# Gates one unit later, keys copied by two engines, and the last tile in two halves of columns, in a two-layer streaming encoder step

## The chip, the cores and the metric

The kernel runs on 1 core of one Trainium2 chip. The metric is the device time in microseconds (us) of one execution; the median over several executions is given. The engines are named as the profile names them: PE is TensorE, PEld its weight loads, DVE is VectorE, ACT is ScalarE, POOL is GpSimd, SP is the engine whose queue issues most DMAs.

## The reference, cut to what matters

```python
def mixer_layer(h, p, pos, ckv_past, krope_past, conv_past, ...):
    z = rmsnorm(h, ln_in) @ w_in
    c_q, c_kv, k_r, g_a, u_val, u_gate, g_c = jnp.split(z, [...], axis=-1)
    q = (rmsnorm(c_q, ln_q) @ w_q_b).reshape(b, t, 8, 96)      # 64 plain + 32 rotated
    ckv_new = rmsnorm(c_kv, ln_kv)
    # keys and values of a head come from ckv_new through w_kv_b; block-causal softmax
    y_a = rmsnorm(o_a * jax.nn.silu(g_a), ln_out_a)
    u = u_val * jax.nn.sigmoid(u_gate)
    v = causal_dwconv(u_pad, conv_w, conv_b)                   # 31 taps
    v = jax.nn.silu(layernorm(v, ln_conv_g, ln_conv_b))
    y_c = rmsnorm(v * jax.nn.silu(g_c), ln_out_c)
    h = h + jnp.concatenate([y_a, y_c], axis=-1) @ w_out
    gate = jax.nn.sigmoid(rmsnorm(h, ln_pg) @ w_pg)
    return h + gate * (p @ w_pe), ckv_new, kr_new, conv_state
# two layers, over a prompt group (512 frames) and a sample group (8 x 16 frames with a
# cache of 256), then y = rmsnorm(h, ln_f)
```

## The kernel before

**Tiles.** The 640 token rows lie in five tiles of 128 (`t` 0 to 3 the prompt, 4 the samples). Each product with a weight matrix is formed in chunks `c` of 256 input rows (two `k` of 128). A weight chunk is split into a high part `WHI` (ACT, `high(i)`) and a low part `WLO` (DVE, `low(i)`), the activations likewise into `XHI` and `XLO`, and `quantum(name, c, t)` issues for each `k` three fp32r matmuls of 128x512 into the bank `acc[t]` (L653, L656, L659). `pg0` and `pg1` are the two column halves of the gate product that ends a layer.

**Shared banks.** All other PE results go through three banks, `sharedS`, `sharedT` and `sharedO`. `shared_bank_plan()` writes out by hand the order in which results occupy each: PE waits with `fill_wait` until the result before it in the same bank is drained, and the engine that copies a result out says so with `drain_inc`.

**The attention stage.** Eight sample steps `s` and then 32 units `u` (head `h` = u // 4, query block `i` = u % 4) run one after the other. In a unit, PE issues `scores(u+1)` into `sharedS` (128x128(i+1) columns, two fp32 instructions, L864), filler (single `k` parts of the products `ga` and `gc`, L653 to L659), `values(u-1)` (L878) and `flip_probs(u)` (transposes, L581). DVE takes the scores out of `sharedS` with `mask` (L1586, `SB,NBIAS<-sharedS`), ACT forms the exponent (L1260, `probs`), copies the transposed block (`PT`, `probs_out`), and where a filler part ends a tile, `block_out` copies it (`H<-acc`; the name H stands for the same memory as Y here) and forms its tanh (`TH`, L1135). DVE's `filler_gate` (L1509) then multiplies the two. Tiles of `gc` end in units 22, 23, 25, 26 and 28. DVE also works off the convolution taps (L1532) between these, and `head_out`, `queries_out` and `conv_stats`.

**Loops around it.** In unit 3, 11 and 19 PE's `keys(h+2)` makes the keys of two heads in one bank, partitions 0 to 63 the one, 64 to 127 the other; ACT's `keys_out` copies both into `KH`, and the next scores wait for that bank. At the last sample step `value_rows(0)`, `value_rows(1)` and `queries(0)` all use `sharedS`.

**The end.** In layer 1 `pg1` is formed for c = 0 for all tiles, then tile by tile for c = 1, 2, 3. For each tile ACT takes the tanh (`pg_out`), DVE gates and adds (`gate_embedding`, L1509 and L1782), ACT sums the squares (`mean_square`, L1040), DVE forms the reciprocal root by eight dependent one-column instructions (`rstd_of_tile`, L1806 to L1810), and ACT and DVE scale a half each (`scaled`), one tile late: `scaled(t-1)` stands behind the gate of tile t. SP then stores the tile.

Of the kernel before, what the change touches and what calls it, by code (L numbers as in the profile page):

```python
# [110 lines left out]
def shared_bank_plan():  # L111
# [16 lines left out]
    for l in range(DEPTH):  # L128
# [38 lines left out]
        for g in range(2):  # L167
            for t in range(TILES):
                cyc((l, ("h", t, g)))
        if l < DEPTH - 1:  # L170
            cyc((l + 1, "gain"))
            for t in range(TILES):
                cyc((l + 1, ("x", t, 0)))
# [3 lines left out]
def build(nc, a):  # L177
    ctx = ExitStack()
    plan = shared_bank_plan()
    with ctx:  # L180
# [109 lines left out]
        piece_used = sem("piece_used")  # L290
        half_hi = sem("half_hi")
        rows_left = sem("rows_left")
        spilled = sem("spilled")
# [27 lines left out]
        lnkv_in = sem("lnkv_in")  # L321
        rope_copied = sem("rope_copied")
        lnf_in = sem("lnf_in")
        lnf_applied = sem("lnf_applied")
# [6 lines left out]
        def bank(name):  # L331
            return shared[plan[name][0]]
# [54 lines left out]
        def split_place(i, low, k, n):  # L387

            if AT_LAST.get(i) == 2:

                return (XHI, XLO)[low][:, 2 * k:2 * k + 2, 0:2, :].rearrange("p t r e -> p t (r e)")
            slot = 0 if AT_LAST.get(i) == 3 else i % SPLIT
            return (WHI, WLO)[low][:, slot, k, 0:n]

        def raw_rows(i, raw, k):
# [180 lines left out]
        def tensor_layer(pe, l):  # L576
# [24 lines left out]
            def turn_small():  # L601
# [306 lines left out]
            flip_cache(1)  # L908
            filler(0, slice(0, 1))
            for s in range(NB):  # L910
# [11 lines left out]
                if s == NB - 1:  # L922
                    keys(0)
                    filler(s, slice(1, 2))
                    value_rows(1)
                    queries(0)
                    filler(s, slice(2, None))
                else:
                    filler(s, slice(1, None))
                if s in (0, 1):  # L930
# [81 lines left out]
            if l == DEPTH - 1:  # L1012

                for t in range(TILES):
                    quantum("pg1", 0, t)
                for t in range(TILES):
                    for c in (1, 2, 3):
                        quantum("pg1", c, t)
                return
            for c in range(4):  # L1020
# [9 lines left out]
        def scalar_layer(act, l, th, n_sq):  # L1030
# [396 lines left out]

            for t in range(TILES):
                pg_out(1, t)
# [6 lines left out]
            if last:  # L1436
                scaled(TILES - 1)

        def vector_layer(dve, l, chain, halves, k_th):
# [176 lines left out]
            for s in range(NB):  # L1616
# [8 lines left out]
                filler_gate(s)  # L1625

            def head_out(h):
                name = ("oh", h)
# [40 lines left out]
            for u in range(UNITS):  # L1669
# [130 lines left out]
            def rstd_of_tile(t):  # L1800
# [4 lines left out]
                dve.wait_ge(squares, SQUARES * DEPTH + TILES + t + 1)  # L1805
                chain.link(tt(x, MS[:, t:t + 1], MS[:, 5 + t:6 + t], ALU.subtract))  # L1806
                chain.link(ts(y.bitcast(I32), x.bitcast(I32), -0.5, MAGIC - 2.0 ** 22 - 2.0 ** 30, ALU.mult, ALU.add))
                for k in range(3):
# [12 lines left out]
            if last:  # L1821
                chain.link(nc.vector.tensor_scalar(MS[:, 0:5], MS[:, 0:5], -1.0, -0.5 * EPS, ALU.mult, ALU.add))
            for t in range(TILES):
                gate_embedding(1, t)
                if last:

                    if t:
                        scaled(t - 1)
                    rstd_of_tile(t)
            if last:  # L1830
                scaled(TILES - 1)

# [142 lines left out]
```

## Time and profile before

| | us |
|---|---|
| median of 3 runs | 790.71 (790.63 to 790.83) |
| the profiled execution | 791.15 |
| its span, first to last instruction | 789.4 |
| PE busy in the span | 765.8 |
| DVE busy | 561.5 |
| ACT busy | 425.2 |
| granted TensorE clock, mean | 0.997 |

A row of the timeline gives the start and the duration of an instruction (or of several alike, xN), and in brackets how long its engine had been idle before it and what ended that. Ends of matmuls are modelled: neighbouring rows of PE overlap, so an idle time in brackets is counted from a modelled end. Starts are what can be subtracted.

### The profile page before, as it was taken

The numbers are of one execution on the slowest core, as the hardware profiler recorded it, in microseconds if no ns is written. First come the engines' busy times: TensorE is split into PE (matmuls) and PEld (weight loads), VectorE is DVE, ScalarE is ACT, GpSimd is POOL, SyncE is SP. The second block draws the span as 40 slices with busy tenths as digits, with TensorE's granted clock in tenths as the row PEclk, the third lists the DMA queues.
The fourth block names the chain that finished last, engine by engine and source line by source line (L and its number), as shares of the span: only waits on it lengthen the run. The fifth ranks groups of instructions, "written<-read, shape, count | busy, mean of one in ns | idle before, by whom it ended". The sixth has DMA issues, their size and how long they took to land.

```text
span 789.4 us, 10538 instructions
## 1 busy us (share of the span) xinstructions
PE 765.8 (97%) x3767; PEld 606.3 (77%) x3767; DVE 561.5 (71%) x1086; ACT 425.2 (54%) x982; POOL 65.0 (8%) x114
## 2 busy tenths in 40 slices
PE   8999999999998999999999999999999899999995
PEld 7799877677766588888888988776777666888874
DVE  3449989877765995646463799897778579656477
ACT  3765656764455653353365484657545558223654
POOL 1400123200000500000000011222000000000000
PEclk9999999999999999999999999999999999999998
DMA  8822222100000354422182323121000004341203
GB/s 269 248 76 81 81 70 84 38 28 27 1 27 1 105 175 145 113 78 81 54 271 58 102 75 91 49 58 28 27 27 28 1 27 139 115 146 54 83 25 134
DMA packets 45833, 65.54 MB, mean 83 GB/s; under 512 B 12590, under 2 KB 24714, under 8 KB 45766
## 3 DMA queue, kind: packets, MB, share of 16 engines
q1 hardware_dynamic: 41946, 58.45, 23.7%
q0 software_dynamic: 3776, 6.40, 2.7%
q8 instruction: 31, 0.51, 0.3%
q14 instruction: 20, 0.16, 0.1%
q10 hardware_dynamic: 60, 0.02, 0.0%
HBM read 57.87 MB, written 7.18 MB: 82 GB/s over the span
## 4 chain that ended last, share of the span: by engine, by line
PE 86%; DVE 7%; ACT 6%; issue 1%; POOL 0%; ACTq 0%; DVEq 0%; POOLq 0%
PE acc L653 19%; PE acc L659 19%; PE acc L656 19%; PE acc L789 4%; PE sharedT L581 4%; PE sharedS L864 4%; PE sharedO L878 3%; PE sharedT L851 3%; PE sharedO L581 2%; PE sharedS L581 2%; PE sharedS L837 1%; PE sharedS L838 1%; DVE VT L1532 1%; PE sharedO L825 1%; ACT KH L1044 1%
## 5 line engine op out<-in xcount | busy, mean ns | idle before, releaser
L653 PE MATMUL acc<-WHI,XHI 128*128 128x512 f32 (+1 forms) x710 | 309.2, 435 | 0.9 <-ACT WHI L1044 0.4
L659 PE MATMUL acc<-WHI,XLO 128*128 128x512 f32 (+1 forms) x710 | 274.8, 387 | 0.0
L656 PE MATMUL acc<-WLO,XHI 128*128 128x512 f32 (+1 forms) x710 | 274.3, 386 | 0.3 <-DVE WLO L1462 0.3
L1532 DVE SCALAR_TENSOR_TENSOR VT<-UX,CWT,VT 128x640 f32<-128x640 f32 x240 | 211.5, 883 | 4.9
L653 PEld LDWEIGHTS acc<-WHI,XHI 128*128 128x128 f32 x710 | 133.8, 188 | 32.8 <-issue 8.7
L656 PEld LDWEIGHTS acc<-WLO,XHI 128*128 128x128 f32 x710 | 134.0, 189 | 30.6 <-issue 8.1
L1462 DVE SCALAR_TENSOR_TENSOR WLO<-WR,GT,WHI 128x512 fp32r<-128x512 f32 (+1 forms) x142 | 98.7, 737 | 79.7 <-ACT WHI L1044 79.0
L659 PEld LDWEIGHTS acc<-WHI,XLO 128*128 128x128 f32 x710 | 133.3, 188 | 26.0
L1044 ACT ACTIVATE WHI<-WR,GT 128x512 fp32r<-128x512 f32 (+1 forms) x142 | 93.4, 709 | 91.2 <-PE acc L659 91.0
L1260 ACT ACTIVATE SB<-SB,NBIAS 128x384 f32<-128x384 f32 (+1 forms) x80 | 45.9, 574 | 47.7 <-DVE NBIAS L1586 47.1
L1044 ACT ACTIVATE PT<-sharedT 128x384 f32<-128x384 f32 (+1 forms) x80 | 35.4, 443 | 45.5 <-PE sharedT L581 45.0
L864 PE MATMUL sharedS<-KH,QH 128*128 128x128 f32 (+3 forms) x128 | 47.1, 450 | 8.2 <-DVE NBIAS L1586 7.1
L878 PEld LDWEIGHTS sharedO<-V,PT 128*128 128x128 f32 x320 | 44.9, 191 | 9.4 <-issue 3.8
L878 PE MATMUL sharedO<-V,PT 128*128 128x128 f32 x320 | 46.4, 275 | 0.3
L1586 DVE CUSTOM_DVE_ANT_0 SB<-sharedS,MASK 128x128 f32<-128x128 f32 (+1 forms) x64 | 31.3, 489 | 19.5 <-PE sharedS L864 19.5
L1040 ACT ACTIVATE JUNK<-H 128x512 bf16<-128x512 f32 (+1 forms) x50 | 39.9, 798 | 7.7 <-DVE H L1782 4.5
L581 PE MATMUL sharedT<-IDENT,SB 128*128 128x128 f32 x208 | 35.8, 273 | 0.7 <-DVE QH L1613 0.7
L789 PE MATMUL acc<-WR,PTR 128*128 128x512 f32 x80 | 36.0, 592 | 0.0
L1135 ACT ACTIVATE TH<-acc,HR 128x512 f32<-128x512 f32 x40 | 27.3, 687 | 9.4 <-PE acc L659 7.5
L1733 DVE SCALAR_TENSOR_TENSOR H<-acc,RS,H 128x512 f32<-128x512 f32 x40 | 28.5, 746 | 3.2 <-PE acc L659 2.8
L864 PEld LDWEIGHTS sharedS<-KH,QH 128*128 128x128 f32 x128 | 19.2, 190 | 12.8 <-DVE NBIAS L1586 9.5
L1044 ACT ACTIVATE XHI<-sharedO 128x512 fp32r<-128x512 f32 x22 | 13.1, 597 | 28.7 <-PE sharedO L581 28.7
(200 smaller groups left out, 864.0 us busy)
## 6 DMA issues: line engine op xcount, KB each, us to landing
WR<-in_w_in_dram SPq DMA_DIRECT2D x32, 256.0 KB, 3.0
WR<-in_w_in_dram SPq DMA_DIRECT2D x16, 512.0 KB, 3.7
WR<-in_w_out_dram SPq DMA_DIRECT2D x16, 512.0 KB, 3.6
WR<-in_w_pg_dram SPq DMA_DIRECT2D x16, 512.0 KB, 3.5
H<-in_x_prompt_dram SPq DMA_DIRECT2D x16, 256.0 KB, 4.9
WR<-in_w_in_dram SPq DMA_DIRECT2D x8, 416.0 KB, 3.8
residual_spill<-H SPq DMA_DIRECT2D x5, 512.0 KB, 4.1
H<-residual_spill SPq DMA_DIRECT2D x10, 256.0 KB, 3.4
```

The costliest lines, as they stand in the source:

```text
L581: return nc.tensor.transpose(out, in_, IDENT[0:rows, 0:rows])
L653: mm(out, hi, w_hi, start=(first and k == 0), stop=False)
L656: mm(out, hi, w_lo, start=False, stop=False)
L659: last = mm(out, lo, w_hi, start=False, stop=(final and k == 1))
L789: last = mm(acc[t][:, :], PTR[:, k, P * t:P * (t + 1)], WR[:, j % RAW, k, :], start=(k == 0), stop=(k == 1))
L864: fill_inc(mm(bank((l, name))[:, 0:w], QH[:, h % 2, P * i:P * (i + 1)], KH[:, h % 3, 0:w], start=True, stop=True), (l, name))
L878: last = mm(quad(name)[:, i, :], PT[:, n % 2, j, :], V[:, j, P * (h // 2):P * (h // 2 + 1)], start=(j == 0), stop=(j == i))
L1040: av(JUNK[:, 0:src.shape[-1]], src, ACT.Square, scale=scale * n ** -0.5, accum_out=MS[:, col:col + 1]).then_inc(squares, 1)
L1044: return av(out, in_, ACT.Copy) if scale is None else av(out, in_, ACT.Copy, scale=scale)
L1260: av(SB[:, n % 2, 0:w], SB[:, n % 2, 0:w], ACT.Exp, scale=-1.0, bias=NBIAS[:, n:n + 1], accum_out=SUMS[:, n:n + 1]).then_inc(exped, 1)
L1462: out = stt(out=split_place(i, 1, k, n), in0=raw_rows(i, raw, k), scalar=gain_column(i, k), in1=split_place(i, 0, k, n).bitcast(F32), op0= ...
L1532: stt(out=out, in0=src, scalar=w, in1=out, op0=ALU.mult, op1=ALU.add).then_inc(conv_done, 1)
```

## The change

It has six parts.

1. In layer 0 the part `u0`, c = 2, tile 0 is issued inside `turn_small`, ahead of the transposes of the convolution state, and left out of its loop.
2. Ahead of sample step 0 two filler parts are issued instead of one, and one fewer in the step.
3. The value rows 1 move from `sharedS` to `sharedO`.
4. Of keys 2, 4 and 6 DVE copies the upper partitions (`second_keys_out`), ACT the lower ones in two pieces of 384 and 128 columns, the second after DVE is through.
5. `filler_gate` of unit u-1 is called in unit u, behind the mask, `head_out`, `queries_out` and the first tap.
6. In layer 1 the last tile of `pg1` is formed in two halves of 256 columns, the second in `sharedS` (`"last"`); tanh, gate, residual and squares are done per half, with one more subtraction in the root.

```diff
-        order["S"] += [(l, ("v", 0)), (l, ("v", 1)), (l, ("q", 0)), (l, ("s", NB)), (l, ("u", 3, 1))]
+        order["S"] += [(l, ("v", 0)), (l, ("q", 0)), (l, ("s", NB)), (l, ("u", 3, 1))]
...
+            if s == NB - 1:
+                order["O"].append((l, ("v", 1)))
             order["O"].append((l, ("o", s)))
...
+                if l == 0:
+
+                    copied_wait(pe, (l, ("x", 0, 1)))
+                    quantum("u0", 2, 0)
                 pe.wait_ge(state_in, 16 * (l + 1))
...
-            filler(0, slice(0, 1))
+            filler(0, slice(0, 2))
...
-                for t in range(TILES):
+                def half_quantum(c, x):
+                    i, t = PART[l, "pg1", c], TILES - 1
+                    out = (acc[t], bank((l, "last")))[x][:, 0:256]
+                    for k in range(2):
+                        hi, lo = XHI[:, t, 2 * c + k, :], XLO[:, t, 2 * c + k, :]
+                        w_hi, w_lo = (split_half(i, low, k, x) for low in (0, 1))
+                        mm(out, hi, w_hi, start=((c, k) == (0, 0)), stop=False)
+                        mm(out, hi, w_lo, start=False, stop=False)
+                        out_ins = mm(out, lo, w_hi, start=False, stop=((c, k) == (3, 1)))
+                    return out_ins
+
+                for t in range(TILES - 1):
                     quantum("pg1", 0, t)
-                for t in range(TILES):
+                pe.wait_ge(acc_drained[TILES - 1], BLK[l, "pg1"])
+                half_quantum(0, 0)
+                fill_wait(pe, (l, "last"))
+                half_quantum(0, 1).then_inc(piece_used, 1)
+                for t in range(TILES - 1):
                     for c in (1, 2, 3):
                         quantum("pg1", c, t)
+                for x in range(2):
+                    for c in (1, 2, 3):
+                        done = half_quantum(c, x)
...
-                copy(KH[0:NOPE, h % 3, :], bank((l, name))[0:NOPE, :])
-                drain_inc(copy(KH[0:NOPE, (h + 1) % 3, :], bank((l, name))[NOPE:P, :]), (l, name))
...
+                copy(KH[0:NOPE, h % 3, 0:384], bank((l, name))[0:NOPE, 0:384])
+
+                act.wait_ge(k_second, (HEADS // 2 - 1) * l + h // 2)
+                drain_inc(copy(KH[0:NOPE, h % 3, 384:512], bank((l, name))[0:NOPE, 384:512]), (l, name))
...
+                if i == 3 and h in (0, 2, 4):
+                    second_keys_out(h + 2)
                 if i == 2 and h < HEADS - 1:
                     queries_out(h + 1)
+
+                if u:
+                    filler_gate(NB + u - 1)
                 taps(TAP.get(NB + u, [])[early:])
-                filler_gate(NB + u)
...
+                for x in range(2):
+                    cols = slice(256 * x, 256 * (x + 1))
...
+                    av(TH[:, k % 2, cols], (acc[t], bank((l, "last")))[x][:, 0:256], ACT.Tanh, scale=HR[:, t:t + 1]).then_inc(half_tanh, 1)
+                    if x == 0:
+                        scaled(t - 1)
+                    act.wait_ge(half_done, x + 1)
+                    mean_square(H[:, t, 512 + 256 * x:768 + 256 * x], 5 + t + x, D, 0.5 ** 0.5)
+                scaled(t)
```

How the instructions stand on DVE in units 22 to 25 (ISA SB,NBIAS is a mask, H<-TH,H a gate, QH the queries, OTOK a head), before:

```order
L1532 SCALAR_TENSOR_TENSOR VT<-UX,CWT,VT 128x5x128
L1613 TENSOR_TENSOR QH<-sharedT,ROPET 128x512
L1509 SCALAR_TENSOR_TENSOR H<-TH,H 128x512
L1586 ISA SB,NBIAS<-sharedS,MASK 128x128
L1586 ISA NBIAS 128x1
L1532 SCALAR_TENSOR_TENSOR VT<-UX,CWT,VT 128x5x128
L1509 SCALAR_TENSOR_TENSOR H<-TH,H 128x512
L1586 ISA SB,NBIAS<-sharedS,MASK 128x256
```

The same place on DVE after:

```order
L1592 SCALAR_TENSOR_TENSOR VT<-UX,CWT,VT 128x5x128
L1673 TENSOR_TENSOR QH<-sharedT,ROPET 128x512
L1646 ISA SB,NBIAS<-sharedS,MASK 128x128
L1646 ISA NBIAS 128x1
L1592 SCALAR_TENSOR_TENSOR VT<-UX,CWT,VT 128x5x128
L1569 SCALAR_TENSOR_TENSOR H<-TH,H 128x512
L1646 ISA SB,NBIAS<-sharedS,MASK 128x256
L1646 ISA NBIAS 128x1
L1592 SCALAR_TENSOR_TENSOR VT<-UX,CWT,VT 128x5x128
L1696 RECIPROCAL RSUM<-SUMS 128x4
L1699 TENSOR_TENSOR OTOK<-sharedO,RSUM 128x4x64
L1569 SCALAR_TENSOR_TENSOR H<-TH,H 128x512
```

Each gate has moved behind the next unit's mask.

DVE at the very end, the last tile of layer 1 (OTOK<-TH is its gate, H<-OTOK the residual, H<-H,RS,KH the scaling, here of the tile before), before:

```order
L1509 SCALAR_TENSOR_TENSOR OTOK<-TH,OTOK 128x512
L1782 SCALAR_TENSOR_TENSOR H<-OTOK,H 128x512
L1818 SCALAR_TENSOR_TENSOR H<-H,RS,KH 128x512
L1806 TENSOR_TENSOR NR<-MS 128x1
L1807 TENSOR_SCALAR RS<-NR 128x1
```

And after:

```order
L1908 SCALAR_TENSOR_TENSOR OTOK<-TH,OTOK 128x256
L1910 SCALAR_TENSOR_TENSOR H<-OTOK,H 128x256
L1891 SCALAR_TENSOR_TENSOR H<-H,RS,KH 128x512
L1908 SCALAR_TENSOR_TENSOR OTOK<-TH,OTOK 128x256
L1910 SCALAR_TENSOR_TENSOR H<-OTOK,H 128x256
L1875 TENSOR_TENSOR NR<-MS 128x1
L1879 TENSOR_TENSOR NR<-NR,MS 128x1
```

On ACT, from the squares of tile 3 to the end (TH is a tanh, JUNK,MS squares, H<-H,RS a scaling), the last rows before are:

```order
L1040 ACTIVATE JUNK,MS<-H 128x512
L1135 ACTIVATE TH<-acc,HR 128x512
L1044 ACTIVATE H<-H,RS 128x512
L1040 ACTIVATE JUNK,MS<-H 128x512
L1044 ACTIVATE H<-H,RS 128x512
```

and after, from the first half's tanh on:

```order
L1492 ACTIVATE TH<-acc,HR 128x256
L1085 ACTIVATE H<-H,RS 128x512
L1081 ACTIVATE JUNK,MS<-H 128x256
L1492 ACTIVATE TH<-sharedS,HR 128x256
L1081 ACTIVATE JUNK,MS<-H 128x256
L1085 ACTIVATE H<-H,RS 128x512
```

The second half's tanh stands behind the first half's squares, and DVE's second gate behind the scaling of tile 3.

## Rows read from the trace of the kernel before

**Rows 1.** The page: busy time of PE, and the TensorE clock in 40 slices.
```profile
PE 765.8 (97%) x3767; PEld 606.3 (77%) x3767; DVE 561.5 (71%) x1086; ACT 425.2 (54%) x982; POOL 65.0 (8%) x114
PEclk9999999999999999999999999999999999999998
```

**Rows 2.** Waits of PE: who was waited for, us in total, times, longest.
```profile
PE sharedS L864 <- DVE NBIAS L1586: 7.1, 10, 0.9
...
PE sharedS L864 <- ACT KH L1044: 1.1, 6, 0.2
```

**Rows 3.** Stretches: length, busy PE, PEld, DVE, ACT, POOL, then PEclk.
```profile
231.50:251.50 20.00, 16.17 (x87) 11.91 (x85) 13.26 (x31) 10.39 (x26) 0.00 (x0) 1.00 0.00 1
...
256.00:480.00 224.00, 223.85 (x1077) 182.97 (x1077) 148.33 (x286) 117.34 (x249) 13.44 (x20) 1.00 0.37 114
```

**Rows 4.** Timeline: PE rows of parts 1 to 4 that stood behind a wait.
```profile
28.88 0.60 PE L581 MATMUL sharedO<-IDENT,VT 120*128 120x120 f32 x4 [0.86 <-DVE XLO L1474]
...
113.89 0.89 PE L837 MATMUL sharedS<-CTK,V 128*128 128x384 f32 x2 [0.43 <-ACT CTK L1044]
...
155.38 1.98 PE L851 MATMUL sharedS<-CQT,WQ 128*128 128x512 f32 x4 [0.69 <-ACT V L1044]
...
175.46 0.70 PE L864 MATMUL sharedS<-KH,QH 128*128 128x256 f32 x2 [0.18 <-ACT KH L1044]
```

**Rows 5.** Timeline: PE's other queries, four instructions without a wait, and ACT's keys.
```profile
168.21 1.88 PE L851 MATMUL sharedT<-CQT,WQ 128*128 128x512 f32 x4
...
174.21 1.20 ACT L1044 ACTIVATE KH<-sharedS 64x512 f32<-64x512 f32 x2 [0.72 <-PE sharedS L845]
```

**Rows 6.** Timeline of units 22 to 24: tanh, gate, mask, and the scores behind them.
```profile
230.62 0.69 ACT L1135 ACTIVATE TH<-acc,HR 128x512 f32<-128x512 f32 x1
...
231.35 0.69 DVE L1509 SCALAR_TENSOR_TENSOR H<-TH,H 128x512 f32<-128x512 f32 x1 [2.45 <-ACT TH L1135]
...
231.96 0.28 DVE L1586 CUSTOM_DVE_ANT_0 SB<-sharedS,MASK 128x128 f32<-128x128 f32 x1
...
232.30 0.70 PE L864 MATMUL sharedS<-KH,QH 128*128 128x256 f32 x2 [0.64 <-DVE NBIAS L1586]
```

**Rows 7.** Groups by line and form: count, busy us, mean ns.
```profile
L1532 DVE SCALAR_TENSOR_TENSOR VT<-UX,CWT,VT 128x640 f32<-128x640 f32 x240 | 211.5, 883 | 4.9
...
L1516 DVE SCALAR_TENSOR_TENSOR H<-TH,H 128x256 f32<-128x256 f32 x20 | 7.7, 421 | 1.0 <-ACT TH L1156 1.0
...
L1509 DVE SCALAR_TENSOR_TENSOR OTOK<-TH,OTOK 128x512 f32<-128x512 f32 x10 | 6.9, 685 | 0.0
...
L1156 ACT ACTIVATE TH<-acc,HR 128x256 f32<-128x256 f32 x20 | 9.6, 482 | 0.0
...
L1040 ACT ACTIVATE JUNK<-Z 128x256 bf16<-128x256 f32 x10 | 4.2, 418 | 0.7
```

**Rows 8.** Timeline of PE: neighbouring matmuls of 416 and of 512 columns.
```profile
48.52 0.35 PE L653 MATMUL acc<-WHI,XHI 128*128 128x416 f32 x1
...
48.71 0.35 PE L656 MATMUL acc<-WLO,XHI 128*128 128x416 f32 x1
...
779.79 0.39 PE L656 MATMUL acc<-WLO,XHI 128*128 128x512 f32 x1
...
780.02 0.39 PE L659 MATMUL acc<-WHI,XLO 128*128 128x512 f32 x1
```

**Rows 9.** Timeline of the last tile, DVE and ACT.
```profile
781.43 0.68 DVE L1509 SCALAR_TENSOR_TENSOR OTOK<-TH,OTOK 128x512 f32<-128x512 f32 x1
...
782.76 0.74 DVE L1818 SCALAR_TENSOR_TENSOR H<-H,RS,KH 128x512 f32<-128x512 f32 x1
782.87 0.63 ACT L1040 ACTIVATE JUNK<-H 128x512 bf16<-128x512 f32 x1 [0.60 <-DVE H L1782]
...
783.63 0.16 DVE L1806 TENSOR_TENSOR NR<-MS 128x1 f32<-128x1 f32 x1
...
785.52 0.75 DVE L1818 SCALAR_TENSOR_TENSOR H<-H,RS,KH 128x512 f32<-128x512 f32 x1
```

More of the change, by code:

```diff
@@ L169, in shared_bank_plan @@
                 cyc((l, ("h", t, g)))
-        if l < DEPTH - 1:
+        if l == DEPTH - 1:
+            order["S"].append((l, "last"))
+        else:
             cyc((l + 1, "gain"))
@@ L291, in build @@
         half_hi = sem("half_hi")
+        half_tanh = sem("half_tanh")
+        half_done = sem("half_done")
         rows_left = sem("rows_left")
@@ L322, in build @@
         rope_copied = sem("rope_copied")
+        k_second = sem("k_second")
         lnf_in = sem("lnf_in")
@@ L393, in split_place, with split_half @@
             return (WHI, WLO)[low][:, slot, k, 0:n]
+        def split_half(i, low, k, x):
+            place = split_place(i, low, k, 512)
+            if AT_LAST.get(i) == 2:
+                return place[:, x, :]
+            return place[:, 256 * x:256 * (x + 1)]
         def raw_rows(i, raw, k):
@@ L715, in tensor_layer @@
             for c in (2, 3):
-                for t in range(TILES):
+                for t in range(1 if (l, c) == (0, 2) else 0, TILES):
                     copied_wait(pe, (l, ("x", t, 1)))
@@ L928, in tensor_layer @@
                 else:
-                    filler(s, slice(1, None))
+                    filler(s, slice(1 if s else 2, None))
                 if s in (0, 1):
@@ L1012, in tensor_layer @@
             if l == DEPTH - 1:
-                for t in range(TILES):
-                    quantum("pg1", 0, t)
-                for t in range(TILES):
+                def half_quantum(c, x):
[9 more added lines that the diff above has]
+                for t in range(TILES - 1):
+                    quantum("pg1", 0, t)
+                pe.wait_ge(acc_drained[TILES - 1], BLK[l, "pg1"])
[3 more added lines that the diff above has]
+                for t in range(TILES - 1):
                     for c in (1, 2, 3):
                         quantum("pg1", c, t)
+                for x in range(2):
+                    for c in (1, 2, 3):
+                        done = half_quantum(c, x)
+                    if x == 0:
+                        done.then_inc(acc_filled[TILES - 1], 1)
+                    else:
+                        fill_inc(done, (l, "last"))
                 return
@@ L1284, in keys_out @@
                 filled_wait(act, (l, name))
-                copy(KH[0:NOPE, h % 3, :], bank((l, name))[0:NOPE, :])
-                drain_inc(copy(KH[0:NOPE, (h + 1) % 3, :], bank((l, name))[NOPE:P, :]), (l, name))
+                if h == 0:
+                    copy(KH[0:NOPE, 0, :], bank((l, name))[0:NOPE, :])
+                    drain_inc(copy(KH[0:NOPE, 1, :], bank((l, name))[NOPE:P, :]), (l, name))
+                    return
+                copy(KH[0:NOPE, h % 3, 0:384], bank((l, name))[0:NOPE, 0:384])
+                act.wait_ge(k_second, (HEADS // 2 - 1) * l + h // 2)
+                drain_inc(copy(KH[0:NOPE, h % 3, 384:512], bank((l, name))[0:NOPE, 384:512]), (l, name))
             def value_rows_out(j):
@@ L1426, in scaled @@
                 copy(H[:, t, 0:512], H[:, t, 0:512], RS[:, t:t + 1]).then_inc(y_ready[0], 1)
-            for t in range(TILES):
+            for t in range(TILES - 1 if last else TILES):
                 pg_out(1, t)
@@ L1436, in scalar_layer @@
             if last:
-                scaled(TILES - 1)
+                t, k = TILES - 1, th[0]
+                act.wait_ge(gated, k - 1)
+                for x in range(2):
+                    cols = slice(256 * x, 256 * (x + 1))
+                    if x == 0:
+                        act.wait_ge(acc_filled[t], BLK[l, "pg1"] + 1)
+                    else:
+                        filled_wait(act, (l, "last"))
+                    av(TH[:, k % 2, cols], (acc[t], bank((l, "last")))[x][:, 0:256], ACT.Tanh, scale=HR[:, t:t + 1]).then_inc(half_tanh, 1)
+                    if x == 0:
+                        scaled(t - 1)
+                    act.wait_ge(half_done, x + 1)
+                    mean_square(H[:, t, 512 + 256 * x:768 + 256 * x], 5 + t + x, D, 0.5 ** 0.5)
+                scaled(t)
         def vector_layer(dve, l, chain, halves, k_th):
@@ L1625, in vector_layer, with second_keys_out @@
                 filler_gate(s)
+            def second_keys_out(h):
+                name = ("k", h)
+                filled_wait(dve, (l, name))
+                nc.vector.tensor_copy(KH[0:NOPE, (h + 1) % 3, :], bank((l, name))[NOPE:P, :]).then_inc(k_second, 1)
             def head_out(h):
@@ L1806, in rstd_of_tile @@
                 chain.link(tt(x, MS[:, t:t + 1], MS[:, 5 + t:6 + t], ALU.subtract))
+                if t == TILES - 1:
+                    dve.wait_ge(squares, SQUARES * DEPTH + TILES + t + 2)
+                    chain.link(tt(x, x, MS[:, 6 + t:7 + t], ALU.subtract))
                 chain.link(ts(y.bitcast(I32), x.bitcast(I32), -0.5, MAGIC - 2.0 ** 22 - 2.0 ** 30, ALU.mult, ALU.add))
@@ L1822, in vector_layer @@
                 chain.link(nc.vector.tensor_scalar(MS[:, 0:5], MS[:, 0:5], -1.0, -0.5 * EPS, ALU.mult, ALU.add))
-            for t in range(TILES):
+            for t in range(TILES - 1 if last else TILES):
                 gate_embedding(1, t)
@@ L1830, in vector_layer @@
             if last:
-                scaled(TILES - 1)
+                t, k = TILES - 1, k_th[0]
+                for x in range(2):
+                    emb = EMB[1][t][:, 256 * x:256 * (x + 1)]
+                    dve.wait_ge(half_tanh, x + 1)
+                    chain.link(stt(out=emb, in0=TH[:, k % 2, 256 * x:256 * (x + 1)], scalar=1.0, in1=emb, op0=ALU.add, op1=ALU.mult))
+                    hh = H[:, t, 512 + 256 * x:768 + 256 * x]
+                    stt(out=hh, in0=emb, scalar=0.5, in1=hh, op0=ALU.mult, op1=ALU.add).then_inc(half_done, 1)
+                    if x == 0:
+                        scaled(t - 1)
+                rstd_of_tile(t)
+                scaled(t)
         def pool_start(pool):
```

## The prediction

> **What bounds the kernel now.** I read the page first: PE is busy 97% of the span, at a granted clock of nine tenths or more in 39 of 40 slices [rows 1]. So a change can gain only where PE stands still, and where the end of the program hangs on something else. The table of waits tells who holds PE up: most of it is ten waits of the scores (L864) for DVE's mask, 7.1 us, and six short ones for ACT's copy of the keys, 1.1 us [rows 2]. The busy time by stretches shows where the ten are: in 231.5 to 251.5 PE is busy 16.17 of 20 us, while from 256 to 480 it is busy 223.85 of 224 [rows 3]. The timeline gives the other waits one by one [rows 4]. The last 9 us are a chain of ACT and DVE behind the last matmul [rows 9].
>
> **What a listed wait is worth.** Ends of matmuls are modelled: two of 512 columns start 0.23 us apart and are drawn 0.39 long [rows 8], so a wait counted from such an end is 0.16 short of the gap between starts. And four query instructions behind a wait are drawn 1.98 long, the same four without one 1.88 [rows 4, 5]: 0.10 for getting going again. A listed wait w costs w + 0.16, and up to 0.10 more.
>
> **Part 1, `u0` ahead of the state's transposes.** The wait of 0.86 for the bank [rows 4] is worth 1.02 to 1.1. The six matmuls put into it take 6 x 0.23 = 1.36, longer than the gap, and are only moved. What waited behind is not late: ACT still has the copies of `uk` to do. Gain 1.0 (0.8 to 1.1).
>
> **Part 2, a second filler part.** The wait of 0.43 [rows 4] is worth 0.59, and a part of 3 x 0.23 = 0.68 covers it. Later in step 0 there is one part less ahead of the exponent, which by then is long done. Once per layer: 2 x 0.6 = 1.2 (0.6 to 1.3).
>
> **Part 3, value rows 1 in `sharedO`.** The queries (L851) wait 0.69 because value rows 1, just before them in `sharedS`, are being copied [rows 4]. In the new order the result before them in `sharedS` is value rows 0, copied long before. The new neighbour in `sharedO` is the sample output of step 6, which ACT copies ahead of both. Worth 0.69 + 0.16 = 0.85 per layer, 1.7 (1.3 to 1.9). The query product on DVE follows PE and comes earlier with it.
>
> **Part 4, keys.** Now two ACT copies in a row, 1.20 us [rows 5], hold the bank, and the next scores wait 0.18 [rows 4], worth 0.34, six times [rows 2]. After, ACT's 384 columns and DVE's 512 run side by side. A DVE instruction of 512 columns takes 0.69, one of 256 0.42 [rows 7]; DVE's is done 0.75 after the keys, then ACT's 128 columns, which by the 128-wide to 512-wide slope of its rows is about 0.27: 1.0 in place of 1.2. So 0.2 x 6 = 1.2. It is between 0 (DVE comes late: it still has a tap of 0.88 [rows 7] behind its mask) and 2.0 (the whole gap). The copy of 0.65 that DVE gets is followed by two taps, so the next mask is 0.3 later; the unit behind it is long enough to hide that.
> No row shows two engines reading one bank at once. The Trainium skill ("PSUM — Partial Sum Buffer", section "PSUM bank collisions raise a hardware error") says that different 32-partition quadrants of one bank can be used by two engines together, which is the case here; by it the 1.2 stands, and if they took turns the term would be about -1.
>
> **Part 5, gates one unit later.** This is the large term. Rows of units 22 to 24 show the mechanism: the tanh ends at 231.31, the gate that waited 2.45 us for it starts at 231.35, the mask behind it at 231.96, and the scores that wait for the mask at 232.30 [rows 6]. The scores that this mask reads had been ready since 229.9. DVE, in order, held a ready mask behind a gate whose tanh comes last on ACT. After the change the mask stands ahead of that gate.
> What is taken away: 20.00 - 16.17 = 3.83 us idle per layer in the stretch [rows 3], in six gaps, each 0.16 to 0.26 larger than drawn: 3.8 + 6 x 0.26 = 5.4.
> What is late next: I laid out units 22 to 31 with the rows' durations. PE starts scores(25) at 231.50, scores(26) at 233.6. On DVE, mask(25) runs at 232.1, then a tap, the head, gate(23) (its tanh ends at 233.5), and a second tap till 235.4; only then mask(26), which could have run at 234.4. So scores(27) wait till 236.0, where PE is ready at 235.4: a new gap of 0.6 + 0.1. From there on every mask, exponent and transposed block comes in time, also those of units 29 to 31, where ACT has the convolution's copies as well. 5.4 - 0.7 = 4.7, and small gaps of 0.1 to 0.2 before `values`, which are no row of the waits, go in part: 4.9 per layer, 9.8 in all. Ends: if only half of the gaps go, 2 x 2.5 = 5; if all, 2 x 5.6 = 11.2. The TH buffers are no new wait, since a tanh needs the gate before the last. Behind the stretch, PE runs without a gap to 480 [rows 3], and the convolution's norm, the heads and the residual loads hang on work that moves with it, so the gain is kept.
>
> **Part 6, the last tile in halves.** I expect this one to cost. The last matmul starts at 780.02 [rows 8], and the tanh of 512 would be there at 781.14, but DVE's gate starts only at 781.43, when the root of tile 3 is through [rows 9]: the end hangs on the chain of DVE and ACT, not on PE. Before: gate 781.43, residual, squares 782.87, root from 783.63, scaling 785.52 [rows 9]; the scaling of tile 3 (782.76) lies under ACT's squares. After, in the order that front shows: gate 0 781.43, residual 0 done 782.31 (0.42 each [rows 7], 0.04 between), scaling of tile 3 till 782.97, now with nothing under it; ACT squares half 0 782.35 to 782.9 (0.42 plus the read of the sum), and only then its tanh of half 1, 0.48 [rows 7], till 783.3; gate 1 and residual 1 till 784.2; squares of half 1, root from 784.8. The additional subtraction runs before that sum is there. 784.8 - 783.63 = 1.15 later. So +1.15 (0.8 to 1.8).
> PE doesn't decide it: 96 columns less make a matmul 0.04 shorter (0.19 against 0.23 apart [rows 8]), so 256 columns take about 0.12, an estimate from these two; 12 a quantum instead of 6 cost 0.08 each, 0.3 in all, and PE ends 2 us ahead of need.
> The rows say that two DVE instructions of 256 cost 0.84 where one of 512 costs 0.69 [rows 7]. The Trainium skill ("VectorE: DVE Perf Modes", section "The TRN2 errata — SBUF-src ops pay a fixed extra latency per instruction") advises against it, with tiles of 512 elements or more; by its table a pair of halves costs 0.06 more, by the rows 0.15, and neither changes the sign.
>
> **Sum.** 1.0 + 1.2 + 1.7 + 1.2 + 9.8 - 1.15 = 13.75 off the profiled execution's 791.15: 777.4. That execution is 0.44 above the median of 790.71, so I predict 777.0.
>
> **Rivals.**
> A. Half of part 5 comes back: DVE is 13.3 of 20 us busy in the stretch [rows 3], and a gate that still waits for its tanh between a mask and the next holds the next one. For it: my own layout has one such place. Against: it has only one in ten. 4.9 less: 781.9. Chance 0.13.
> B. The tail gains instead of losing, if DVE's wait for the root of tile 3 is shorter than drawn and the halves overlap: at best the second half's chain is 0.3 (tanh 0.69 to 0.48, and squares) and 0.5 (gate and residual) shorter. With all waits gone: 777.0 - 1.15 - 0.8 = 775.0. Chance 0.08.
> C. A matmul of 256 fp32r columns costs as much as the plain fp32 ones do, 1.88 / 4 = 0.47 for 512 [rows 5], so 0.24 for 256: 36 x 0.24 = 8.5 in place of 4.1 after c = 0, PE ends 4.4 later at 784.8, tanh of half 1 at 785.3 in place of 783.3: +2.0, 779.0. Inside the range, 0.05.
> D. The other side, slower: with its gaps gone PE is granted less clock in one of the stretches of units. At 1.2 GHz in place of 2.4 its 20 us there take 20 more: 777.0 + 20 = 797. It decides from 14 us of PE time at the lower level. Against: the clock is 1.00 both in the stretch with gaps and in 224 us without one [rows 3]. Chance 0.02.
> E. The change doesn't do what it says in the one place where it could fail, the gate's new place: another queue entry ahead of the mask (`head_out`, which waits for PE's values) takes the gate's part. All of part 5 would go, 786.8. Against: `head_out` stood there before. Chance 0.03.
>
> **How the numbers follow.** The forecast as it stands, with the ends of its terms, holds 0.69: the sum of likely small ends is about 10.5 (780.2), of large ones about 16 (774.7). With B and C inside and part of A, 774.6 to 781.0 leaves out about 0.2. A measurement of this kernel can tell about 0.2%, 1.6 us. All cases but D are faster by more: faster 0.96, same 0.02, slower 0.02.
>
> **What would show it.** In the profile after: the waits of L864's successor for NBIAS fall from ten to about two; the waits at 28.9, 113.9 and 155.4 are gone; the key waits are 0.1 or none; the mask of unit 24 starts 0.05 after its scores; and from the gate of the last tile to the last scaling it takes 5.2 us in place of 4.1. Wrong would be: new waits of PE for ACT's `PT` or for DVE's queries in units 23 to 31, or gaps behind 256 that weren't there.

## The result, and the profile after

The changed kernel takes 778.46 us (median of 4 runs, 778.33 to 778.59) against 790.77 for the kernel before beside it (4 runs, 790.63 to 790.91): a ratio of 0.9843, 95% interval 0.9828 to 0.9859. The forecast was 777.0, in a range of 774.6 to 781.0. The gain of 1.6% is clear of the interval. The profiled execution took 778.38 us, its span 776.6; that of before 791.15 and 789.4. One execution of the kernel called x9 below took 1572.03 us, twice the others, and its time there is that of the other three.

The page after; its PE and clock lines answer to [rows 1]:

```profile
PE 762.0 (98%) x3791; PEld 607.3 (78%) x3791; DVE 565.7 (73%) x1095; ACT 422.4 (54%) x985; POOL 65.1 (8%) x114
...
PEclk9999999999999999999999999999999999999998
```

The span is 12.8 us shorter with 24 more matmuls. PE's idle time fell by 9.0, and its busy time by 3.8. I put that down to how a wait is drawn, since instructions behind one are drawn longer than the same in a row [rows 4, 5]; the 3.8 as a whole is not shown to be that. The granted clock is the same, 0.9 or more in 39 of 40 slices, so the upper of its two levels.

PE's waits after, answering to [rows 2] (out, line, who was waited for, us in total, times, longest):

```profile
PE sharedO L842 <- ACT PT L1085: 1.2, 2, 0.6
...
PE sharedS L881 <- DVE NBIAS L1646: 1.1, 2, 0.6
```

L881 is the scores' new line. Its ten waits of 7.1 us for the mask are two, one in each layer; the six waits for the keys and two of 0.7 in all for DVE's queries have left the table; and one stands there that was not in it before: the sample outputs wait for `PT`, 0.6 in each layer.

**Where the 12.8 went.** I cut both traces at marks that PE passes in every version, so that each stretch holds the same work. Times between starts, in us:

| stretch on PE | before | after | change |
|---|---|---|---|
| span's start to the transposes of `uk`, layer 0 | 27.36 | 27.20 | -0.16 |
| to the first scores of sample step 0 | 83.62 | 82.58 | -1.04 |
| to queries 0 | 44.40 | 43.58 | -0.82 |
| to the heads of the sample group | 99.46 | 93.97 | -5.49 |
| to the state transposes of layer 1 | 159.25 | 159.20 | -0.05 |
| to the first scores of sample step 0, layer 1 | 82.03 | 82.05 | +0.02 |
| to queries 0 | 44.46 | 43.63 | -0.83 |
| to the heads of the sample group | 99.46 | 93.96 | -5.50 |
| to the last scaling (DVE) | 145.48 | 146.56 | +1.08 |

They add up to -12.79. The stretches that the change doesn't touch agree within 0.05 us, so this ledger shows effects of a tenth, which the medians can't. Its first line is the exception: over all fourteen profiled kernels that start varied from 26.47 to 27.41 with no edit ahead of it, so a difference of up to 0.9 us between two executions can be start-up and no effect of an edit.

### The profile page after: what moved, and what is told of

Same layout as the page of the kernel before. It is cut to its first block, busy times and chain, and to the rows that moved or that the text cites. A ratio compares the mean times of both kernels' runs of the same rounds, so it can differ in the third digit from the quotient of the medians.

```text
span 776.6 us, 10600 instructions
## 1 busy us (share of the span) xinstructions
PE 762.0 (98%) x3791; PEld 607.3 (78%) x3791; DVE 565.7 (73%) x1095; ACT 422.4 (54%) x985; POOL 65.1 (8%) x114
## 4 chain that ended last, share of the span: by engine, by line
PE 90%; DVE 5%; ACT 3%; issue 1%; POOL 0%; DVEq 0%; ACTq 0%; POOLq 0%
PE acc L670 19%; PE acc L676 19%; PE acc L673 19%; PE sharedT L594 5%; PE acc L806 4%; PE sharedS L881 4%; PE sharedO L895 4%; PE sharedT L868 3%; PE sharedO L594 2%; PE sharedS L594 2%; PE sharedS L854 1%; PE sharedS L855 1%; PE sharedO L842 1%; PE sharedS L862 1%; DVE H L1851 1%
## 5 line engine op out<-in xcount | busy, mean ns | idle before, releaser
L881 PE MATMUL sharedS<-KH,QH 128*128 128x128 f32 (+3 forms) x128 | 46.3, 443 | 1.1 <-DVE NBIAS L1646 1.1
L1081 ACT ACTIVATE JUNK<-H 128x512 bf16<-128x512 f32 (+2 forms) x51 | 40.1, 787 | 8.1 <-DVE H L1851 3.9
L1085 ACT ACTIVATE XHI<-sharedT 128x512 fp32r<-128x512 f32 x19 | 11.3, 596 | 30.5 <-PE sharedT L594 30.5
```

The costliest lines, as they stand in the source:

```text
L881: fill_inc(mm(bank((l, name))[:, 0:w], QH[:, h % 2, P * i:P * (i + 1)], KH[:, h % 3, 0:w], start=True, stop=True), (l, name))
L1081: av(JUNK[:, 0:src.shape[-1]], src, ACT.Square, scale=scale * n ** -0.5, accum_out=MS[:, col:col + 1]).then_inc(squares, 1)
L1085: return av(out, in_, ACT.Copy) if scale is None else av(out, in_, ACT.Copy, scale=scale)
```

## The rows that changed

**Gates.** Units 25 to 27 after, the place that answers to [rows 6] (tanh, gate, masks, taps, scores):

```profile
228.77 0.60 PE L881 MATMUL sharedS<-KH,QH 128*128 128x256 f32 x2
...
229.41 0.42 DVE L1646 CUSTOM_DVE_ANT_0 SB<-sharedS,MASK 128x256 f32<-128x256 f32 x1
...
230.04 0.69 ACT L1176 ACTIVATE TH<-acc,HR 128x512 f32<-128x512 f32 x1
...
230.90 0.81 PE L881 MATMUL sharedS<-KH,QH 128*128 128x384 f32 x2
...
231.40 0.68 DVE L1569 SCALAR_TENSOR_TENSOR H<-TH,H 128x512 f32<-128x512 f32 x1
...
232.00 0.88 DVE L1592 SCALAR_TENSOR_TENSOR VT<-UX,CWT,VT 128x640 f32<-128x640 f32 x1
...
232.80 0.55 DVE L1646 CUSTOM_DVE_ANT_0 SB<-sharedS,MASK 128x384 f32<-128x384 f32 x1
...
233.41 0.70 PE L881 MATMUL sharedS<-KH,QH 128*128 128x512 f32 x1 [0.57 <-DVE NBIAS L1646]
```

The mask of unit 25 starts 0.04 after its scores end (229.37), where a gate with its tanh still to come used to stand ahead of it. The scores of unit 26 end at 231.71, but their mask starts only at 232.80, behind a gate and a tap, and the scores of unit 27 wait 0.57 for it: the wait that was laid out, at its place. It is not new, though. Before, the same scores waited 0.56, with no gate but a head and a tap ahead of the mask. A little later in that trace, PE's transposes waited for the queries on DVE, which stood behind a late gate, its mask and a tap:

```profile
238.15 1.13 PE L864 MATMUL sharedS<-KH,QH 128*128 128x512 f32 x2 [0.56 <-DVE NBIAS L1586]
...
243.14 0.52 PE L581 MATMUL sharedT<-IDENT,SB 128*128 128x128 f32 x3 [0.33 <-DVE QH L1613]
```

**Keys.** Timeline after, answering to [rows 5] and the last of [rows 4]:

```profile
172.09 0.48 ACT L1085 ACTIVATE KH<-sharedS 64x384 f32<-64x384 f32 x1 [0.73 <-PE sharedS L862]
172.09 0.69 DVE L1690 COPY KH<-sharedS 64x512 f32<-64x512 f32 x1 [0.46 <-PE sharedS L862]
...
172.82 0.27 ACT L1085 ACTIVATE KH<-sharedS 64x128 f32<-64x128 f32 x1 [0.24 <-DVE KH L1690]
...
173.14 0.70 PE L881 MATMUL sharedS<-KH,QH 128*128 128x256 f32 x2
```

ACT and DVE start at 172.09 on the same bank, one on each half of its partitions, and take their usual time. The last copy ends at 173.09, 1.00 after the first began, where two copies in a row took 1.20.

**State and values.** PE's rows after at the first and the third of [rows 4]: the transposes into `sharedO` come behind the moved quantum, the queries straight behind value rows 1, both without a wait.

```profile
29.09 0.57 PE L594 MATMUL sharedO<-IDENT,VT 120*128 120x120 f32 x4
...
152.50 1.02 PE L904 MATMUL sharedO<-WKV,CKVT 128*128 128x512 f32 x2
153.36 1.88 PE L868 MATMUL sharedS<-CQT,WQ 128*128 128x512 f32 x4
```

**The last tile.** DVE and ACT after, answering to [rows 9] (L1908 gates, L1891 scalings, JUNK squares, L1879 the new subtraction ahead of the root):

```profile
767.50 0.42 DVE L1908 SCALAR_TENSOR_TENSOR OTOK<-TH,OTOK 128x256 f32<-128x256 f32 x1
...
768.29 0.74 DVE L1891 SCALAR_TENSOR_TENSOR H<-H,RS,KH 128x512 f32<-128x512 f32 x1
768.41 0.42 ACT L1081 ACTIVATE JUNK<-H 128x256 bf16<-128x256 f32 x1
768.82 0.45 ACT L1492 ACTIVATE TH<-sharedS,HR 128x256 f32<-128x256 f32 x1
769.31 0.43 DVE L1908 SCALAR_TENSOR_TENSOR OTOK<-TH,OTOK 128x256 f32<-128x256 f32 x1 [0.27 <-ACT TH L1492]
...
770.84 0.16 DVE L1879 TENSOR_TENSOR NR<-NR,MS 128x1 f32<-128x1 f32 x1 [0.58 <-ACT JUNK L1081]
...
772.73 0.75 DVE L1891 SCALAR_TENSOR_TENSOR H<-H,RS,KH 128x512 f32<-128x512 f32 x1
```

From the gate to the last scaling it is 5.23 us, against 785.52 - 781.43 = 4.09 [rows 9]. The second tanh stands behind the first half's squares, DVE waits 0.27 for it, and then 0.58 for the second squares.

## The experiments

The large term comes first, alone and undone; then the tail; then the part that fell short and what the profile showed in its place. Ratios are against the kernel before, run beside them (791.01 to 791.21 us).

**Part 5 alone, and all but part 5.** The edit, added to before (x1) or taken from after (x2):

```
             if i == 2 and h < HEADS - 1:
                 queries_out(h + 1)
+            if u:
+                filler_gate(NB + u - 1)
             taps(TAP.get(NB + u, [])[early:])
-            filler_gate(NB + u)
```

> The kernel before with part 5 alone (each gate of a filler tile one unit later). Theory: the gates held ready masks back, and that was most of the time that PE stood still; the offset between the two traces grows by 4.8 us in units 22 to 31 of each layer, so 790.8 - 9.6 = 781.2 us. Rival: part of this comes from DVE having less to do or being earlier through the other parts; then this kernel gives clearly less, 784 or more.

> The changed kernel with part 5 alone undone. Theory: 778.5 + 9.6 = 788.1 us, and the ten waits of the scores for the mask are back. Rival as for the kernel with the gates alone: if the other parts share in the gain, 785 or less.

Measured: x1 781.47 us (780.59 to 781.72), ratio 0.9881 [0.9865, 0.9897]; x2 788.34 (788.30 to 788.45), 0.9967 [0.9954, 0.998]. x1's profiled execution began 0.8 early (26.54 against 27.36), which the ledger leaves out: added alone, the stretches with the units are 4.83 and 4.80 shorter; taken away, 4.82 and 4.89 longer. PE's wait in x2 and in x1:

```profile
PE sharedS L881 <- DVE NBIAS L1646: 7.1, 10, 0.9
```

```profile
PE sharedS L864 <- DVE NBIAS L1586: 1.1, 2, 0.6
```

Busy time in the stretch 228 to 250 us (length, then PE, PEld, DVE, ACT, POOL, clock, share and GB/s of the DMAs) of x2 and of x1:

```profile
228.00:250.00 22.00, 18.14 (x98) 13.36 (x97) 13.42 (x31) 12.17 (x31) 0.00 (x0) 1.00 0.00 1
```

```profile
228.00:250.00 22.00, 21.43 (x137) 17.65 (x135) 15.68 (x36) 14.79 (x37) 0.00 (x0) 1.00 0.00 1
```

So the place of one DVE instruction in the order of a unit makes eight of the ten waits, and nothing else in the change does; the two of 0.57, one per layer, stay with either place. DVE's and ACT's busy time rises with PE's, as the same work is packed closer. Rival A (half comes back) and E (another entry takes the gate's part) are out: both runs measure about 9.7 us.

**Part 6: the last tile whole again (x3), and in halves in another order (x4).** x3 puts back the code of before for that tile. x4 keeps the halves and moves two things:

```
 ACT:  for x in range(2):
           wait for half x; tanh of half x
-          if x == 0: scaled(t - 1)
-          squares of half x
+      scaled(t - 1)
+      for x in range(2): squares of half x
       scaled(t)
 DVE:  gate 0, residual 0
-      scaled(t - 1)
       gate 1, residual 1
+      scaled(t - 1)
```

> The changed kernel with part 6 alone undone: the last tile in one piece. Theory: the halves cost what the chain of DVE and ACT got longer, 1.1 us, so 777.4 us, and from the last gate to the last scaling it takes 4.1 us again. Rival: the halves gain at PE what they lose in the chain: 778.5 or more.

> The changed kernel, still with two halves, but ACT takes both tanhs before the scaling of tile 3 and both squares, and DVE gates and adds both halves before its scaling of tile 3. Theory: the loss comes from the places of the scaling and of the second tanh, not from the number of instructions; root from 2.3 us after the first gate in place of 3.3, so 777.5 us. Rival: it comes from the fixed cost of two more instructions on each engine (0.15 a pair on DVE, more on ACT); then 0.3 to 0.5 us of the 1.1 come back, 778.0.

Measured: x3 777.48 us (777.21 to 777.92), 0.983 [0.9815, 0.9845]; x4 777.74 (777.52 to 777.77), 0.9832 [0.9818, 0.9847]. The last stretch of the ledger: after 146.56, x3 145.43, x4 145.67. The halves cost 1.13, and the reordering gets back 0.89 of it. The median of x4 lies between the 777.5 expected and the rival's 778.0, so it is the ledger that decides. x4's DVE:

```profile
767.76 0.42 DVE L1908 SCALAR_TENSOR_TENSOR OTOK<-TH,OTOK 128x256 f32<-128x256 f32 x1
...
768.55 0.42 DVE L1908 SCALAR_TENSOR_TENSOR OTOK<-TH,OTOK 128x256 f32<-128x256 f32 x1
...
770.01 0.15 DVE L1875 TENSOR_TENSOR NR<-MS 128x1 f32<-128x1 f32 x1
770.20 0.16 DVE L1879 TENSOR_TENSOR NR<-NR,MS 128x1 f32<-128x1 f32 x1
...
772.09 0.75 DVE L1891 SCALAR_TENSOR_TENSOR H<-H,RS,KH 128x512 f32<-128x512 f32 x1
```

The second gate follows 0.79 behind the first instead of 1.81. What the halves cost is thus mostly the scaling of tile 3 and the first squares put between them. Of the 0.24 that are left, 0.19 is the additional subtraction of the root (L1879), which here stands in the chain: from the root's first instruction to the scaling it is 2.08 us, against 785.52 - 783.63 = 1.89 before [rows 9]. The doubled instructions of gate, residual and squares come to 0.05.

**Part 2: the second filler part undone (x5).**

```
-            filler(0, slice(0, 2))
+            filler(0, slice(0, 1))
...
-                    filler(s, slice(1 if s else 2, None))
+                    filler(s, slice(1, None))
```

> The changed kernel with part 2 alone undone (one filler part ahead of sample step 0). Theory: part 2 gained nothing, since the chain of ACT from the cache's copy to the copy of the transposed block sets the time of step 0: 778.5 us, the wait of 0.43 before the scores of step 1 is back and the wait of 0.62 for PT is gone. Rival: part 2 gained its 1.2 us and the wait for PT has another cause, one that the earlier state of layer 0 brings: 779.7 us.

Measured: 778.42 us (778.33 to 778.47), 0.9838 [0.9823, 0.9853]. Undoing the part costs next to nothing: the stretches around step 0 are 82.61, 43.65 and 82.03, 43.66, against 82.58, 43.58 and 82.05, 43.63. At most 0.1 us in each layer where I had 0.6. The wait for `CTK` is back in x5's table,

```profile
PE sharedS L854 <- ACT CTK L1085: 0.9, 2, 0.4
```

and the waits for `PT` are gone from it. The part moved a wait of PE by 6 us and made it no shorter. Step 0 before, ACT with the sample outputs that read `PT`:

```profile
115.79 0.95 ACT L1044 ACTIVATE CTK<-sharedT 128x256 f32<-128x256 f32 x3 [1.31 <-PE sharedT L581]
116.76 1.34 ACT L1044 ACTIVATE WHI<-WR,GT 128x512 fp32r<-128x512 f32 x2
...
119.85 0.51 ACT L1044 ACTIVATE PT<-sharedT 128x384 f32<-128x384 f32 x1
...
120.51 0.68 PE L825 MATMUL sharedO<-PT,V 128*128 128x128 f32 x4
```

And after:

```profile
118.68 0.51 ACT L1085 ACTIVATE PT<-sharedT 128x384 f32<-128x384 f32 x1
...
119.33 0.68 PE L842 MATMUL sharedO<-PT,V 128*128 128x128 f32 x4 [0.62 <-ACT PT L1085]
```

Before, `PT` was ready at 120.36 and PE came at 120.51: 0.15 of slack. ACT's chain to it starts from PE's transposes of the cache and runs 4.6 us through the copies, the weight split and the convolution's copies. The part moved ahead of the scores is one part less between those transposes and the outputs, so PE arrives 0.7 earlier relative to the chain, and the slack of 0.15 becomes a wait.

**ACT's split behind the copy of `PT`, in step 0 (x6).** If it is ACT's chain, shortening it ahead of `PT` by the split's 1.33 should give part 2 its gain.

```
-            split_high(s)
+            if s:
+                split_high(s)
             ...
             probs_out(s, 3)
+            if s == 0:
+                split_high(s)
```

> The changed kernel with ACT's split of a weight chunk (WHI, two instructions, 1.3 us) of sample step 0 moved behind the copy of the transposed block PT. Theory: ACT's chain in step 0 is 1.2 us shorter, the wait of 0.62 for PT goes, twice: 778.5 - 2 x 0.7 = 777.1 us. Rival: the chain hangs on another instruction (the turned u in sharedO, or the transposes), and the wait stays or turns up elsewhere: 778.5 us.

Measured: 777.97 us (777.49 to 779.22), 0.9838 [0.9821, 0.9854]. The wait for `PT` is gone, so the chain is shown. But the gain is 0.21 and 0.35 in the two layers in place of 0.7 each, so the time lies between the theory's and the rival's: another wait has come up a little later.

```profile
124.84 0.41 PE L594 MATMUL sharedT<-IDENT,V 128*128 128x128 f32 x2 [0.32 <-DMA CKR<-in_cache_krope_dram]
```

**Unit 24's second tap moved to unit 28 (x7).** The one mask that is still late has a gate and a tap ahead of it. In the tuple that deals out the taps, unit 24 gets one in place of two, and unit 28 gets the other:

```
-(..., 1, 1, 1, 1, 2, 1, 1, 2)
+(..., 1, 1, 1, 1, 1, 1, 1, 2, 1)
```

> The changed kernel with one of the two taps of unit 24 moved to a unit with none: the taps of units 25 to 28 each shift by one. Theory: the wait of 0.57 that is left in the units comes from the gate and the second tap between mask 25 and mask 26 on DVE; without that tap mask 26 starts 0.8 earlier and the wait goes, twice: 778.5 - 2 x 0.65 = 777.2 us. Rival: mask 26 waits for the gate's tanh rather than for the tap: 778.4 us.

Measured: 776.56 us (776.46 to 777.11), 0.9816 [0.9802, 0.9831]. The stretches with the units are 0.83 and 0.76 shorter than after's, a little more than the listed 0.57 + 0.16, so the tap is what held that mask. The same window for x7:

```profile
228.00:250.00 22.00, 21.92 (x141) 18.11 (x141) 16.98 (x38) 15.48 (x39) 1.11 (x2) 1.00 0.01 2
```

PE is now busy in 21.92 of 22 us, with four instructions more in it than x1 had: the stretch of [rows 3] is full.

**Parts 4, 3 and 1 undone, one at a time (x9, x10, x11).** x9 has both key copies on ACT; x10 puts value rows 1 back into `sharedS`; x11 puts the quantum back behind the state's transposes.

```
x9   -  DVE copies KH from the bank's second half, ACT the rest in two pieces
     +  copy(KH[0:NOPE, h % 3, :], bank((l, name))[0:NOPE, :])
     +  drain_inc(copy(KH[0:NOPE, (h + 1) % 3, :], bank((l, name))[NOPE:P, :]), (l, name))
x10  -  if s == NB - 1: order["O"].append((l, ("v", 1)))
     -  order["S"] += [(l, ("v", 0)), (l, ("q", 0)), ...]
     +  order["S"] += [(l, ("v", 0)), (l, ("v", 1)), (l, ("q", 0)), ...]
x11  -  if l == 0: copied_wait(pe, (l, ("x", 0, 1))); quantum("u0", 2, 0)
```

> The changed kernel with part 4 alone undone (ACT copies both halves of the keys). Theory: the offset between the traces grows by 0.19 us at each of the six places: 778.5 + 1.1 = 779.6 us. Rival: the copies on two engines gain only what DVE loses elsewhere: 778.5 us.

> The changed kernel with part 3 alone undone (value rows 1 in sharedS). Theory: the wait of 0.69 before the queries is back in both layers, 0.93 each with the restart: 778.5 + 1.9 = 780.3 us. Rival: only the drawn wait counts, 0.69 each: 779.8 us.

> The changed kernel with part 1 alone undone. Theory: the wait of 0.86 is back in layer 0 only, 1.2 by the offset between the traces: 779.7 us. Rival: part of the offset has another cause in the first 30 us, as arrival of the inputs: 779.3 us or less.

| undone | median, us | ratio [95%] | stretches that grew |
|---|---|---|---|
| part 4 (x9) | 778.95 | 0.9849 [0.9829, 0.9868] | heads +0.54, +0.57 |
| part 3 (x10) | 780.36 | 0.9862 [0.9847, 0.9876] | queries +0.85, +0.85; heads +0.08, +0.08 |
| part 1 (x11) | 779.35 | 0.985 [0.9836, 0.9865] | first scores, layer 0, +1.02 |

Each brings back its own wait and moves nothing else behind the start-up by over 0.12. Two of the medians don't choose between theory and rival, and the ledger does: x9's 778.95 lies between 779.6 and 778.5, and its two stretches grew by 0.19 a place. In x11 the rival holds: of the 1.2 that I had read from the offset between the traces, 0.16 lies in the start-up, and the part is worth 1.0. The waits in x9 (table), x10 and x11 (timeline) are those of before to the digit:

```profile
PE sharedS L881 <- ACT KH L1085: 1.1, 6, 0.2
```

```profile
154.46 1.98 PE L866 MATMUL sharedS<-CQT,WQ 128*128 128x512 f32 x4 [0.69 <-ACT V L1083]
```

```profile
28.90 0.60 PE L594 MATMUL sharedO<-IDENT,VT 120*128 120x120 f32 x4 [0.86 <-DVE XLO L1530]
```

**The three edits together (x8: x3, x6 and x7), and the loads in another order (x12).** x12 is x8 with one more edit: POOL issues the two loads of `CKR` of a step first, once PE has transposed that slot, and the load of `V` behind them.

```
+            if s >= CACHED:
+                filled_wait(pool, (l, ("c", s - CACHED)))
             the two loads of CKR
+            if s >= CACHED:
+                filled_wait(pool, (l, ("o", s - CACHED)))
             the load of V
 ahead of the whole step:
-    filled_wait(pool, (l, ("o", s - CACHED)))
```

> The changed kernel with the last tile in one piece, the split of step 0 behind the copy and the tap of unit 24 moved. Theory: the three add up: 778.5 - 1.1 - 1.4 - 1.3 = 774.7 us, and PE has no wait over 0.3 us between 12 us and the last gate product. Rival: a further wait takes their place: 776 us or more.

> The kernel with the three edits together, and of each later cache load POOL now issues the two rotary parts (CKR) first, as soon as PE has turned the entry whose place they take, and only the latents (CKV) after the sample output. Theory: in the kernel with the three edits PE waits 0.47 and 0.28 us for the second CKR load, the last of three issues of 0.72 us each that all stood behind the sample output; with one issue left there the waits go: 775.1 - (0.47 + 0.28 + 2 x 0.16) = 774.0 us. Rival: the latents' own landing is as late, and the wait only changes its name: 775.0 us.

Measured: x8 775.10 us (775.01 to 775.15), 0.9796 [0.9782, 0.9811]; x12 774.17 (774.05 to 774.25), 0.9785 [0.9772, 0.9799]. x8's stretches are those of its three edits added, to within 0.1. The 774.7 expected was missed by 0.4, since x6's edit gives 0.6 where 1.4 had been put in, and x7's 1.6 where it was 1.3. Nor is PE free of waits over 0.3. Its POOL and PE show why the `CKR` wait is there, now at 0.47:

```profile
119.69 0.77 POOL L499 DMA_DIRECT2D V<-in_cache_ckv_dram  x1 [10.28 <-PE sharedO L841]
120.46 1.46 POOL L503 DMA_DIRECT2D CKR<-in_cache_krope_dram  x2
...
125.37 0.41 PE L592 MATMUL sharedT<-IDENT,V 128*128 128x128 f32 x2 [0.47 <-DMA CKR<-in_cache_krope_dram]
```

POOL waits for the outputs that read the slot's `V`, and the two `CKR` issues stand behind it, though their place in the slot is free sooner; the last is issued by 121.92 and PE wants it at 124.9. x12's POOL issues them 11 us earlier:

```profile
109.60 1.50 POOL L503 DMA_DIRECT2D CKR<-in_cache_krope_dram  x2
119.93 0.72 POOL L507 DMA_DIRECT2D V<-in_cache_ckv_dram  x1 [8.82 <-PE sharedO L845]
```

The waits for them are gone, and 0.62 and 0.40 with them. The edit changes the order of the loads and what they wait for at once, and no run parts the two. What x12's PE still waits for:

```profile
PE acc L703 <- POOL TH L1871: 1.1, 1, 1.1
PE acc L672 <- ACT WHI L1063: 0.4, 1, 0.4
PE acc L675 <- DVE WLO L1490: 0.3, 1, 0.3
PE acc L672 <- DVE WLO L1490: 0.3, 1, 0.3
```

No wait of the scores, the outputs or the queries is left; x12 is 4.3 us faster than the changed kernel, and 2.15% under before.

## Why the prediction held, point by point

| part | forecast | measured | from |
|---|---|---|---|
| 1, `u0` ahead of the transposes | 1.0 | 1.0 | ledger, x11 |
| 2, second filler part | 1.2 | 0.1 | x5 |
| 3, value rows 1 in `sharedO` | 1.7 | 1.9 | x10 |
| 4, keys by two engines | 1.2 | 1.1 | x9 |
| 5, gates one unit later | 9.8 | 9.7 | x1, x2 |
| 6, last tile in halves | -1.15 | -1.1 | ledger, x3 |

The measured terms add up to 12.7; the spans are 12.8 apart.

**Part 5** came to its size, with the wait that is left at the place laid out for it. Before and x1 have the same instructions of PE in the same order, so the offset between the two traces can be read at each. In either layer it grows by 0.91, 1.10, 0.92 and 1.12 at the four scores that waited 0.64, 0.84, 0.65 and 0.85, so 0.27 above each listed wait; by 0.49 at the transposes that waited 0.33 for the queries; and by 0.25 at one `values` without a listed wait. Together that is 4.8. At the fifth of the scores, where before has 0.56 and x1 0.57, it doesn't grow: the forecast called this wait new, but had also taken it out with the six gaps, so the sum was right. The queries are what the ten listed waits for the mask leave out: they hung on the same gates. DVE's own wait at the gates for their tanh, which held the masks, is 2.45 at its longest before [rows 6] and 0.5 after.

**Part 3** gave 0.85 per layer as worked out, and 0.08 more behind it, which was not in the sum. **Part 4** took a fifth of a us off each copy: ACT and DVE read one bank side by side, in 0.48 and 0.69 us. The Trainium skill ("PSUM — Partial Sum Buffer", section "PSUM bank collisions raise a hardware error") says that two engines can access different quadrants of one bank at the same time. The trace agrees. **Part 1** is its wait plus 0.16.

**Part 2 is the step that failed.** It said: "Later in step 0 there is one part less ahead of the exponent, which by then is long done." The exponent was long done: before, it ends at 114.5, and PE's transposes of it start at 118.1. But the part less also stood ahead of PE's sample outputs, and their operand `PT` was ready only 0.15 us before PE. I looked at one consumer behind the moved work, and not at each. A gain of 1.2 became one of 0.1. The forecast did name waits for `PT` as a sign of being wrong, but in units 23 to 31; they came in step 0. Nor was this the last limit: with ACT's chain shortened (x6), the loads of `CKR` were late by 0.3.

**Part 6** cost what its layout said. The rows of the lengths 0.42 and 0.48 were enough, since the term comes from the order of the instructions.

**The numbers.** With part 2 at 0.1 the sum would have been 12.65, so 778.5 for the profiled execution, which took 778.38. The other 0.4 is the offset that I took off: the profile of before lay 0.4 above its median, and that of after at its median. The start-up stretch alone varies by more than that between executions, so an offset of one profile should not have been carried to another. Beside the later runs the median of the kernel before was 791.0 to 791.2, so the 0.4 was no steady difference between profile and median.

**The rivals.** A fell for the reason given against it: one new wait per layer and no more (1.1 us in both). B was wrong in sign. C: the matmuls of 256 columns at the end of PE's work after:

```profile
762.28 0.28 PE L1039 MATMUL acc<-WHI,XHI 128*128 128x256 f32 x1
...
762.39 0.28 PE L1040 MATMUL acc<-WLO,XHI 128*128 128x256 f32 x1
```

They start 0.11 apart, not 0.24. D: the clock is 1.00 in the stretch with no gaps, x7's included. E: x1 shows the gate's new place working alone.

## What to carry to other kernels

When an engine works in order, look for a result that another engine waits for behind an instruction whose own operand comes late; moving the late one behind it gave 9.7 us here and brought PE no new wait. Before filling a gap with work taken from later, write down for every consumer that this work stood ahead of how early its operand is: where the smallest of these margins is 0.15, as here, the gain can't be more, and the gap only moves. Splitting the last tile cost time in both orders that were run, 1.1 us with the first half's follow-up in the second half's way and 0.2 with it behind.

## What the runs showed of the hardware that was not expected

- The time from the span's start to the first transposes of `uk` varied between executions from 26.47 to 27.41 us for the same code up to there. Where single executions differ by under 1 us, that stretch has to be set aside; marks inside the traces told apart a tenth.
- Three load issues on POOL took 0.72 to 0.77 us each, one after the other, so the last was through 2.2 us after the first began. Issued 11 us earlier, the two loads of `CKR` no longer made PE wait the 0.47.
- Effects of these edits add up almost exactly: part 5 alone gives 4.83 and 4.80, with all others around it 4.82 and 4.89.
